# Two-layer diffusion backbone: the first projection starts on half of the features, with the modulation chunks and their turns reordered around it

## The reference, cut to what matters

```python
def rms_norm(x, g):
    y = x * lax.rsqrt(jnp.mean(x * x, axis=-1, keepdims=True) + NORM_EPS)
    return y * g

def modulate(h, shift, scale):
    return h * (1.0 + scale) + shift
...
    for l in range(DEPTH):                       # DEPTH = 2
        sh1, sc1, g1, sh2, sc2, g2 = jnp.split((silu_c @ ada_w[l] + ada_b[l])[:, None, :], ADA_CHUNKS, axis=-1)
        csh1, csc1, cg1, csh2, csc2, cg2 = jnp.split(silu_cc @ ada_w[l] + ada_b[l], ADA_CHUNKS, axis=-1)
        h = modulate(rms_norm(x, norm1_g[l]), sh1, sc1)
        hc = modulate(rms_norm(xc, norm1_g[l]), csh1, csc1)
...
    qa, ka, va, qb, kb, vb = jnp.split(t @ w_in, EVEN_SPLITS, axis=-1)      # 1024 x 3072, t = h and hc
```

## Time and profile before

| | us |
|---|---|
| median of 3 runs | 1859.13 |
| lowest and highest | 1858.90, 1860.81 |
| the profiled execution's own time | 1860.53 |
| its span in the trace | 1858.7 |
| busy: PE, DVE, ACT, POOL | 1819.7, 1381.6, 1114.9, 207.3 |
| DMA, whole program | 496.43 MB, mean 267 GB/s |

### The profile page before, as it was taken

How to read it: one execution, slowest core, us unless ns; L and a number is a source line. 1 busy time by engine, 2 the same in 40 slices (tenths; PEclk the granted TensorE clock), 3 DMA queues, 4 the chain that set the end, 5 groups by cost and what they waited for, 6 DMA issues and landing times.

```text
span 1858.7 us, 25142 instructions
## 1 busy us (share of the span) xinstructions
PE 1819.7 (98%) x8852; PEld 1452.5 (78%) x8852; DVE 1381.6 (74%) x1730; ACT 1114.9 (60%) x1531; POOL 207.3 (11%) x269
## 2 busy tenths in 40 slices
PE   7999989999999999999999999999999999999999
PEld 3777657888888886658888887888888888888877
DVE  3633685777556664543898998999999899899887
ACT  3523674322222223574788887778788787877775
POOL 1317230011001102440100000000000000000010
PEclk9999999999999999999999999999999999999999
DMA  9446202696545451220999999999999999999995
GB/s 357 149 154 205 101 1 91 217 330 233 178 150 181 164 176 43 100 83 9 352 383 360 387 385 359 381 366 386 392 371 390 370 373 389 371 386 379 374 391 214
DMA packets 234933, 496.43 MB, mean 267 GB/s; under 512 B 6128, under 2 KB 44016, under 8 KB 234864
## 3 DMA queue, kind: packets, MB, share of 16 engines
q1 hardware_dynamic: 231328, 488.53, 72.0%
q0 software_dynamic: 1920, 5.77, 1.0%
q10 hardware_dynamic: 1616, 1.22, 0.2%
HBM read 475.05 MB, written 20.45 MB: 267 GB/s over the span
## 4 chain that ended last, share of the span: by engine, by line
PE 77%; DMA 9%; DVE 6%; ACT 4%; issue 3%; POOL 1%; DVEq 0%; ACTq 0%; SPq 0%; POOLq 0%
PE ps L2390 7%; PE ps L2392 7%; PE ps L2391 7%; DMA ring<-in_moe_w 7%; PE ps L2196 7%; PE ps L2198 6%; PE ps L2197 6%; PE ps L2404 4%; PE ps L2402 4%; PE ps L2403 4%; DVE wlo L1759 3%; PE ps L2047 2%; PE ps L1988 2%; PE ps L1990 2%; PE ps L1989 2%
## 5 line engine op out<-in xcount | busy, mean ns | idle before, releaser
L1759 DVE TENSOR_TENSOR wlo<-ring,whi 128x1024 fp32r<-128x1024 f32 x672 | 792.3, 1225 | 89.5 <-ACT whi L1264 82.8
L1264 ACT ACTIVATE whi<-ring 128x1024 fp32r<-128x1024 f32 x672 | 684.2, 1055 | 189.3 <-DMA ring<-in_moe_w 112.3
L2390 PE MATMUL ps<-whi,xgr 128*128 128x512 f32 x896 | 353.4, 394 | 0.1
L2392 PE MATMUL ps<-whi,xgr 128*128 128x512 f32 x896 | 349.4, 390 | 0.0
L2391 PE MATMUL ps<-wlo,xgr 128*128 128x512 f32 x896 | 348.7, 389 | 0.0
L1181 ACT ACTIVATE fsa<-ring 128x1024 fp32r<-128x1024 f32 (+2 forms) x73 | 68.7, 943 | 255.3 <-PE ps L2198 254.3
L2392 PEld LDWEIGHTS ps<-whi,xgr 128*128 128x128 f32 x896 | 168.1, 188 | 35.7
L2391 PEld LDWEIGHTS ps<-wlo,xgr 128*128 128x128 f32 x896 | 168.4, 188 | 33.7
L2390 PEld LDWEIGHTS ps<-whi,xgr 128*128 128x128 f32 x896 | 168.3, 188 | 33.8 <-issue 0.5
L2402 PE MATMUL ps<-whi,hidr 128*128 128x512 f32 x448 | 176.0, 393 | 0.0
L2404 PE MATMUL ps<-whi,hidr 128*128 128x512 f32 x448 | 174.6, 390 | 0.0
(11 more groups left out here) (328 smaller groups left out, 2788.3 us busy)
## 6 DMA issues: line engine op xcount, KB each, us to landing
ring<-in_moe_w SPq DMA_DIRECT2D x168, 2048.0 KB, 10.0
ring<-in_ada_w SPq DMA_DIRECT2D x24, 2048.0 KB, 8.3
ring<-in_ev_w_in SPq DMA_DIRECT2D x6, 2048.0 KB, 10.5
ring<-in_ffn_w_gate SPq DMA_DIRECT2D x11, 1024.0 KB, 5.7
ring<-in_ffn_w_up SPq DMA_DIRECT2D x11, 1024.0 KB, 8.2
expert_tokens<-scr SPq DMA_DIRECT2D x4, 1536.0 KB, 14.6
ring<-in_ffn_w_down SPq DMA_DIRECT2D x4, 1536.0 KB, 6.6
ring<-in_ffn_w_down SPq DMA_DIRECT2D x4, 1280.0 KB, 6.1
```

What stands on the lines that cost most here:

```text
L1264: act.activation(whi[:, u % URING, :], mslot[(u // 4) % MRING][:, (u % 4) * UNIT:(u % 4 + 1) * UNIT], ACT.Copy).then_inc(m_hi, 1)
L1759: dve.tensor_tensor(wlo[:, u % URING, :], mslot[(u // 4) % MRING][:, (u % 4) * UNIT:(u % 4 + 1) * UNIT], whi[:, u % URING, :].bitcast(F32) ...
L2390: pe.matmul(bank[:, :], xgr[:, 0, kk, :], hi[:, ws], start=(kk == 0), stop=False)
L2392: ins = pe.matmul(bank[:, :], xgr[:, 1, kk, :], hi[:, ws], start=False, stop=(kk == KT - 1))
```

## The change

The list of loads is now A0a 0, A0a 2, W0 0, A0a 1, A0a 3, W0 1, A0b 0, A0b 1 and on as before; the slots are given by a table from the first load on. Everything that belongs to feature tiles 0 to 3 is done first: PE takes chunks A0a 0 and 2, turns both, and DVE forms half of the factors. The inverse roots are taken per half of the tokens, 256 columns at a time. The first four units take k = 0 to 3 of units 0 and 1, then chunk A0a 1, k = 0 and 1 of units 2 and 3, chunk A0a 3, k = 2, both turns, k = 3, and after that k = 4 to 7 of units 0 and 1 and of units 2 and 3. POOL's first eight tiles are k = 0 to 3 of both token halves, the other eight wait for the second half of the factors (`ada_rd` 12). The high and low parts of W0 1 move from between the unit follow-ups to this place: its first piece stands ahead of the second-half tokens, the other three behind them. The DMAs of `vec` and `rtr` stand behind the copy of the fourth modulation rows. `busy_tokens` is called once, with 3, instead of with 4, 3 and 3.

```diff
+        order = [("A0a", 0), ("A0a", 2), ("W0", 0), ("A0a", 1), ("A0a", 3), ("W0", 1), ("A0b", 0), ("A0b", 1)]
...
-        L0_SLOTS = [0, 1, 2, 2, 0, 2, 1, 2, 0, 2, 1, 2] + [0, 1, 3, 2]
+        L0_SLOTS = [1, 3, 0, 2, 3, 1] + [2, 2, 0, 2, 1, 2, 0, 2, 1, 2] + [0, 1, 3, 2]
...
-        for j in range(4):
-            released[at["A0a", j]] = (ada_used, j + 1)
+        for n, j in enumerate((0, 2, 1)):
+            released[at["A0a", j]] = (ada_used, n + 1)
...
+        def n00_nth(c, k):
+
+            return 8 * (k // 4) + 4 * c + k % 4
...
-            pool.wait_ge(ada_rd, 2)
...
+            for h in range(2):
+                for c in range(2):
+                    for k in range(4 * h, 4 * h + 4):
+
+                        pool.wait_ge(ada_rd, 3 + 4 * c + k if h == 0 else 12)
...
+            ada_rows(0)
+            ada_rows(1)
+            for k in range(4):
                 if k % 2 == 0:
                     weights_hi(0, k // 2)
                 tokens_hi(0, k)
-            for k in range(KT):
-                tokens_hi(1, k)
+            tokens_hi(1, 0)
+            tokens_hi(1, 1)
+            ada_rows(2)
+            tokens_hi(1, 2)
+            tokens_hi(1, 3)
+            weights_hi(0, 2)
+            weights_hi(0, 3)
+            ada_rows(3)
+            act.dma_start(vec[:, :], a["vec"].partition_broadcast(P)).then_inc(s_vec, 16)
+            act.dma_start(rtr[:, :, :], a["moe_router"].rearrange("(k p) n -> p k n", p=P)).then_inc(s_vec, 16)
+            weights_hi(1, 0)
+            for c in range(2):
+                for k in range(4, KT):
+                    tokens_hi(c, k)
+            for i in range(1, 4):
+                weights_hi(1, i)
...
-                if x % 4 in (1, 2) and c < 5:
+                if x % 4 in (1, 2) and 1 <= c < 5:
...
+            dve.wait_ge(norm["n00"]["root"], 1)
+            ch.after(dve.reciprocal(rstd[:, 0:S_LAT], rt[:, 0:S_LAT]))
+            ada_half(0)
+            factor_half(0)
+            by_root(0)
+            ch.after(dve.reciprocal(rstd[:, S_LAT:S_ALL], rt[:, S_LAT:S_ALL]))
+            by_root(1)
...
+            for k in range(4, KT):
+                ins = dve.tensor_tensor(h0raw[:, k, :], xT[:, k, :], rstd[:, 0:S_ALL], ALU.mult)
+            ch.after(ins)
+            weights_lo(0, 2)
+            weights_lo(0, 3)
+            ada_half(1)
+            factor_half(1)
+            weights_lo(1, 0)
+            for c in range(2):
+                for k in range(4, KT):
+                    tokens_lo(c, k)
+            for i in range(1, 4):
+                weights_lo(1, i)
             dve.wait_ge(s_vec, 32)
...
+            def ada_sums(n):
+                if n >= 2:
+                    pe.wait_ge(ada_row, n - 1)
+                ada_chunk(at["A0a", (0, 2, 1, 3)[n]], ps[4 + n % 2])
...
+                ada_sums(0)
+                ada_sums(1)
+                pe.wait_ge(s_cst, 48)
+                ada_turn(0, adar[0], 0)
+                ada_turn(1, adar[1], 16)
                 busy_tokens(3)
+
+            def first_tiles(us, x):
...
+                if x == 0:
+                    for k in range(4):
+                        tiles(0, k)
+                    ada_sums(2)
+                    tiles(1, 0)
+                    tiles(1, 1)
+                    ada_sums(3)
+                    tiles(1, 2)
+                    pe.wait_ge(ada_rd, 1)
+                    ada_turn(2, adar[0], 8)
+                    ada_turn(3, adar[1], 24)
+                    tiles(1, 3)
+                for k in range(4, KT):
+                    tiles(x // 2, k)
```

More of the change, by code:

```diff
@@ L759, in load @@
             def load(g, dst, src, wait=True):
-                if g >= RING and wait:
+                if before(g) is not None and wait:
                     sp.wait_ge(*released[before(g)])
@@ L1115, in _, with ada_rows @@
             root("n00", S_ALL, KT)
[L1116 to L1122, removed]
+            def ada_rows(n):
+                act.wait_ge(ada_used, n + 1)
+                if n >= 2:
+                    act.wait_ge(ada_tr, n - 1)
+                act.activation(adar[n % 2], ps[4 + n % 2][:, :], ACT.Copy).then_inc(ada_row, 1)
             def tokens_hi(c, k):
                 tc = slice(c * S_LAT, (c + 1) * S_LAT)
-                act.wait_ge(norm["n00"]["scaled"], KT * c + k + 1)
+                act.wait_ge(norm["n00"]["scaled"], n00_nth(c, k) + 1)
                 act.activation(hTh[:, k, tc], h0raw[:, k, tc], ACT.Copy).then_inc(norm["n00"]["ready"], 1)
@@ L1956, in ada_turn, with split3x @@
                 ins.then_inc(ada_tr, 1)
+            def split3x(bank, xh, xl, wh, wl, first, last):
+                pe.matmul(bank, xh, wh, start=first, stop=False)
+                pe.matmul(bank, xh, wl, start=False, stop=False)
+                return pe.matmul(bank, xl, wh, start=False, stop=last)
             def busy_tokens(n):
                 for _ in range(n):
-                    pe.matmul(ps[5][:, :], xT[:, 0, 0:P], xT[:, 0, :], start=True, stop=True)
-            def ada_first():
[L1964 to L1973, removed]
-                busy_tokens(3)
+                    pe.matmul(ps[3][:, :], xT[:, 0, 0:P], xT[:, 0, :], start=True, stop=True)
@@ L2013, in proj_pe @@
                         if nm == "L0":
-                            c, side = un["chunk"], us[x:x + 1] if x >= 4 else us[x:x + 2] if x % 2 == 0 else []
-                            for k in range(KT if side else 0):
-                                if x < 4:
-                                    pe.wait_ge(n00_low, KT * (x // 2) + k + 1)
+                            c, ts = un["chunk"], slice(un["t"] * P, (un["t"] + 1) * P)
+                            if x in (0, 2):
+                                first_tiles(us, x)
+                            for k in range(KT if x >= 4 else 0):
                                 if un["t"] == 0 and k % 2 == 0:
```

74 lines of the change are left out of this document (38 added, 36 removed).

## The result

The changed kernel takes 1865.61 us (median of 6 runs, 1863.25 to 1869.07) against 1859.68 for the kernel before, measured beside it (6 runs, 1858.44 to 1862.60). The ratio of the runs is put at 1.0034, 95% interval 1.0024 to 1.0043, which is some 6.3 us more; the two medians lie 5.9 us apart. That is outside the 0.2% within which I would have called it no change. The profiled execution took 1866.81 us with a span of 1865.0.

A forecast was written before the change was run, and what follows sets the result against it. PE was taken as the bound, so unit 4's start sets the time: start -8.6, moved work +5.7, waits +1.8 and +4.0, unit 1's turn -0.2, clock +2.0, together +4.7 on 1859.13: 1863.8 us, range 1860.5 to 1867.0.

The forecast's parts named there:

- rival 2: PE's clock falls a second time, at unit 0's turn: another 2.0 us, time 1865.8 us; chance 0.14.
- the first low stretch: PE's first projection tiles run at the lower clock after the gap ahead of them: +2.0 us, bounds 0 and 3.
- the second low stretch: Lower clock behind the gap at unit 0's turn: 2.0 us, counted only in the case of two clock falls.
- Part 1: First projection matmul on PE starts at 33.8 us instead of 42.44, 8.6 earlier; bounds 33.0 and 35.2.
- The term for POOL: Ahead of the first projection matmul, POOL's tiles hold DVE up by 0.8 of a possible 2.2 us.
- Part 2: Modulation chunks A0a 1 and 3 and their two turns move behind PE's projection start: +5.7 us.
- Part 3: PE waits 1.8 us ahead of k = 4 for the second half of the features; bounds 0.8 and 2.5.
- Part 4: PE waits 4.0 us at unit 0's turn, behind a chain of 18.3 us from the fourth turn.
- Part 5: PE's clock falls over a 6.1 us gap ahead of the first tile: +2.0 us, bounds 0 and 3.
- unit 1's turn: PE's turn for unit 1, ahead of unit 4, takes 0.44 us instead of 0.64: -0.2 us.
- that PE keeps its rate: PE's clock holds over the gap ahead of the first tile: time 1861.8 us; chance 0.24.
- The faster one: Chain from fourth turn to unit 0's gain shrinks below 12.4 us, both PE waits vanish: down to 1855.3 us; chance 0.07.

The follow-up runs named there:

- the last experiment: Changed kernel with context roots behind the latent low parts, third and fourth turns earlier, W0 1 pieces spread among unit follow-ups: 1854.56 us, ratio 0.9976 to before.

## Why the prediction was right, and where it was off

The direction and the range were right (1863.8, 1860.5 to 1867.0, measured 1865.6). Of the cases it is **rival 2, the clock falling twice, that came true**, at almost its own time, 1865.8; the forecast had it falling once. That the number came out so near is in part luck: the start (0.6 us earlier than predicted), the moved work (0.3 less), the wait at k = 4 (0.3 less) and the first low stretch (0.5 less) were each put too high, while 0.8 us too little was put for the second low stretch and nothing for the cuts in the tiles, 0.8 us. The chances that the prediction adds up for "slower", 0.42, 0.14, 0.05 and 0.03, make 0.64 and not the 0.60 that it states. By its parts:

- **Part 1, the start.** Predicted 33.8 with bounds of 33.0 and 35.2, measured 33.19. The chain is the one that was written down, root by root. The term for POOL was too big: POOL's first four tiles ran in 2.76 us, and they and the next ones stretched DVE's multiplications by some 0.3 us in all, not 0.8. The context roots as the cause are shown by the experiment that moved them.
- **Part 2, the moved work.** Predicted 5.7, measured 2 x 1.85 + 1.69 = 5.4. A term was missing: at each place where the tiles are cut by other work the first matmul behind the cut takes longer. Behind a modulation chunk it is 0.43 in the chain instead of 0.23 (at 42.22 and 47.06), behind the wait at k = 4 0.50 (in the chain of the kernel with the second gap filled), behind the turns 0.32 from start to start (50.20 to 50.52). The four cuts come to some 0.8 us.
- **Part 3, the wait at k = 4.** Predicted 1.8, measured 1.5. The turns ended at 50.35. That it hangs on the turns and on too little work behind them is shown by the kernel with the turns earlier.
- **Part 4, unit 0's turn.** Predicted 4.0, measured 3.99, and the chain from the fourth turn to there 18.3 against 68.5 - 50.35 = 18.2. That the three weight pieces make it is shown by the kernel that moves them.
- **Part 5, the clock.** This is the step that was off. The prediction let PE idle for 6.1 us ahead of the first tile; it was 4.1, since three fillers take 2.8 us and not 1.3 (a row of before had them at 2.82) and the first tile came 0.6 earlier, and the clock fell nevertheless. The low level lasted 3.1 us there and cost 1.5, not 2.0. Having taken the fall for likely at 6.1 us only, I gave the second gap, of 4.0 us, a small chance. It fell there in every kernel that kept it. The low rate then hit a modulation chunk and two turns: 1.11 + 3.57 + 0.89 instead of 0.44 + 1.85 + 0.44, 2.8 us; with that gap filled they took 3.10, so 2.5 of it is shown to be the clock's.

The sum with the measured terms: start -9.25, moved work +5.4, the wait at k = 4 +1.5, unit 0's turn +4.0, first low stretch +1.5, second +2.8, unit 1's turn -0.2, and some 0.8 for the cuts, together +6.6 against 6.66 in the trace.

The rivals: that PE keeps its rate is refuted by the granted clock. The faster one named the right condition. It wanted the chain behind the fourth turn below the work that PE has in the meantime; the change does not do that, and the last experiment, which does but for a wait of 0.5 us, is the one that comes out faster. POOL alone could not have brought it, as said; the order on DVE and ACT could.

The Trainium skill's page TensorE: Matmul & The Clock Gate, section HAM oscillation — how this bites in real kernels, which the prediction applied to the gap ahead of the first tile alone, would have put both gaps among those that cost the clock. Here it went so, at 4.1 and 4.0 us.

## What to carry to other kernels

Starting an engine earlier on half of its data was worth nothing by itself here: ask what each consumer of the last half then has left to hide the chain that leads to it, and count what stands ahead of that chain on every engine's queue. Here 9.3 us were won at the start and 16 were paid behind it: 5.4 for work that only moved, 5.5 for waits, 4.3 for a clock that fell at two gaps of 4 us, 0.8 for the cuts in the tiles. Each of the two gaps cost another 1.5 to 2.8 us behind it, and filler matmuls in both brought unit 4 3.9 us forward.

## What the runs showed of the hardware that I had not expected

- Gaps of PE of 4.0, 4.1 and 4.8 us were each followed by the lower clock level (granted clock 0.50 to 0.64 in the stretches behind that are shown or were read), in five kernels ahead of the first tile and in four ahead of unit 0's turn. Gaps of 1.5, 1.4 us and below were not, in the same stage. Nothing between the two was tried.
- The length of a single gap does not settle it. In the trace of the kernel of before without its last filler the clock fell again in a later stage: 0.67 from 796 to 798 us and 0.50 from 798 to 800. PE's last waits ahead of that were 0.9 and 1.2 us. The kernel of before has the same waits there and keeps 1.00. It cost 1.6 us: four matmuls (L2067) took 2.08 us instead of 1.13 and eight behind them (L2086) 1.70 instead of 1.09.
- So single traces do not speak for all runs of a kernel. Two of the ten runs with both gaps filled have a mean clock of 0.998, where the trace has 1.000, and they are the two slowest, 1865.4 and 1865.8 us. Two of the eleven runs of the last kernel have 0.998 too, without being its slowest. Where the clock fell in them is not recorded.
- The clock did not always fall within the gap. In the changed kernel it did, but with only the first gap filled it stood at 1.00 through the whole gap ahead of unit 0's turn (63.8 to 67.8): the first turn still took 0.66 us, as in the kernel that kept its clock, and the chunk behind it 3.51. PE worked at the low level for some 3 us (0.50 from 42.7 to 45.6) up to 5.3 us (0.52 in the mean from 68.5 to 74.0).
- The same norm sums at the program's start end anywhere between 20.5 and 22.4 us, in the one trace of each of ten kernels in which they are the same instructions. They start at the low rate. A single trace's absolute times are therefore uncertain by up to two microseconds, and positions are better counted from a common event behind it. The 30 runs of before beside the later experiments lie between 1856.67 and 1863.27 us; how much of that comes from the start is not shown.
- DVE's reciprocal did not hold POOL up. Of POOL's first four tiles in the changed kernel, 2.76 us in all, the first took some 1.1 us, mostly beside DVE's multiplications, and the other three some 0.55 each, nearly all beside the reciprocal, which is what a tile takes while DVE is idle; the next four, beside multiplications and low parts, took 6.14 us.
